# Two trunk layers in split float32: four plain feature tiles instead of six, the pre-norm of the other half in nine slots, the convolution's input moved

## What is computed

```python
for i in range(DEPTH):
    hn = rmsnorm(x, mix_pre_g[i])
    y = pool_mixer(hn, ...) if i % 2 == 0 else mlstm_mixer(hn, ...)
    x = x + rmsnorm(y, mix_post_g[i])
    hn = rmsnorm(x, ffn_pre_g[i])
    a = jax.nn.relu(hn @ mlp_w1[i])
    x = x + rmsnorm((a * a) @ mlp_w2[i], ffn_post_g[i])
```

## Time and profile before

| | |
|---|---|
| median of 3 runs | 1963.46 us (1962.75 to 1964.49) |
| the profiled execution | 1964.01 us |
| its span, first to last instruction | 1962.2 us |
| TensorE matmul, weight load | 1926.7 us (98%), 1542.1 us (79%) |
| VectorE, ScalarE, POOL | 1344.6 us (69%), 1067.7 us (54%), 89.9 us (5%) |
| granted TensorE clock, mean | 0.993 |

### The profile page before, as it was taken

How to read it: one execution, slowest core, us unless ns; L and a number is a source line. 1 busy time by engine, 2 the same in 40 slices (tenths; PEclk the granted TensorE clock), 3 DMA queues, 4 the chain that set the end, 5 groups by cost and what they waited for, 6 DMA issues and landing times. The chain is left out here.

```text
span 1962.2 us, 24457 instructions
## 1 busy us (share of the span) xinstructions
PE 1926.7 (98%) x8526; PEld 1542.1 (79%) x8526; DVE 1344.6 (69%) x2120; ACT 1067.7 (54%) x1825; POOL 89.9 (5%) x121
## 2 busy tenths in 40 slices
PE   9999999999999999999999999999999999999999
PEld 6678888888788788778878778877888888878876
DVE  5777565655678977775866766777665656577885
ACT  7655555553445446666655656745645455435433
POOL 0110000000000100110000110011000000000010
PEclk9999999999999999999999999999999999999999
DMA  5344343447633633342323343235334345753353
GB/s 210 109 163 155 118 177 118 177 179 298 214 92 92 200 106 106 110 151 87 99 85 97 111 147 100 83 119 185 115 146 149 146 149 215 294 187 97 103 188 128
DMA packets 79706, 285.00 MB, mean 145 GB/s; under 512 B 9408, under 2 KB 9536, under 8 KB 71136
## 3 DMA queue, kind: packets, MB, share of 16 engines
q1 hardware_dynamic: 64288, 239.96, 34.9%
q0 software_dynamic: 8320, 27.27, 4.3%
q10 hardware_dynamic: 6976, 16.21, 2.8%
HBM read 211.51 MB, written 71.89 MB: 144 GB/s over the span
## 5 line engine op out<-in xcount | busy, mean ns | idle before, releaser
L1821 DVE TENSOR_TENSOR w_lo<-raw,w_hi 128x1024 fp32r<-128x1024 f32 x132 | 162.6, 1232 | 152.6 <-ACT w_hi L1281 150.2
L1467 ACT CAST h_hi<-h_raw 128x512 fp32r<-128x512 f32 x188 | 116.5, 620 | 246.7 <-PE core L1022 149.1
L803 PE MATMUL bank<-x_hi,w_hi 128*128 128x512 f32 x560 | 228.5, 408 | 1.7 <-issue 1.2
L1281 ACT CAST w_hi<-raw 128x1024 fp32r<-128x1024 f32 x132 | 137.6, 1043 | 163.4 <-PE bank L805 52.3
L805 PE MATMUL bank<-x_hi,w_lo 128*128 128x512 f32 x560 | 223.4, 399 | 0.0
L804 PE MATMUL bank<-x_lo,w_hi 128*128 128x512 f32 x560 | 222.2, 397 | 0.0
L2076 DVE TENSOR_TENSOR h_lo<-h_raw,h_hi 128x512 fp32r<-128x512 f32 x188 | 129.8, 690 | 120.8 <-ACT h_hi L1467 120.5
L1020 PE MATMUL core<-h_hi,w_hi 128*128 128x512 f32 x464 | 183.3, 395 | 0.6 <-DVE y L2142 0.6
L1021 PE MATMUL core<-h_lo,w_hi 128*128 128x512 f32 x464 | 183.5, 396 | 0.0
L1022 PE MATMUL core<-h_hi,w_lo 128*128 128x512 f32 x464 | 183.3, 395 | 0.0
L1970 DVE TENSOR_TENSOR w_lo<-sums,w_hi 128x512 fp32r<-128x512 f32 x104 | 71.8, 690 | 100.4 <-ACT w_hi L1309 97.5
(11 more groups left out here) (334 smaller groups left out, 4411.2 us busy)
## 6 DMA issues: line engine op xcount, KB each, us to landing
raw<-weights SPq DMA_DIRECT2D x132, 512.0 KB, 3.3
h_pair_dram<-y SPq DMA_DIRECT2D x26, 1792.0 KB, 6.7
h_raw<-h_pair_dram SPq DMA_DIRECT2D x182, 256.0 KB, 2.8
w<-second_pairs SPq DMA_DIRECT2D x24, 768.0 KB, 4.4
raw_odd<-first_pairs SPq DMA_DIRECT2D x14, 1024.0 KB, 7.1
x_scratch<-y POOLq DMA_DIRECT2D x48, 256.0 KB, 2.5
raw<-first_pairs SPq DMA_DIRECT2D x12, 1024.0 KB, 7.1
xold<-x_scratch POOLq DMA_DIRECT2D x40, 256.0 KB, 3.5
```

Source lines behind the costliest of these rows:

```text
L803: nc.tensor.matmul(o, a, hi(t), start=(k == 0), stop=False)
L1281: nc.scalar.copy(w_hi[:, ROW[u] * T:(ROW[u] + 2) * T], raw[:, (n % RAW) * BLK:(n % RAW + 1) * BLK]).then_inc(hi_ready, 1)
L1467: nc.scalar.copy(h_slot(n)[0], h_raw[:, at % H_RAW, :]).then_inc(h_hi_ready, 1)
L1821: dve.tensor_tensor(w_lo[:, s], raw[:, (n % RAW) * BLK:(n % RAW + 1) * BLK], w_hi[:, s].bitcast(F32), ALU.subtract).then_inc(lo_ready, 1)
```

## The change

Six tiles become four, thirteen pairs fourteen. The chain's slots move from 1 to 11 to 0 to 8; the sums of the input quadrants move with the shorter front; the sets of banks for odd and even pairs are swapped; the early weights of the second product go to the other buffer. In the heads, `conv_input(j, 1)` goes right behind `decay_matrix(j - 1)`, block (j,3) is cast ahead of `query(j)`, and VectorE does `conv(j, 1)` ahead of that block's low part. In the second product, the chain for the MLP's half 0 starts one step earlier and its last part takes three iterations.

```diff
-PLAIN = 6
+PLAIN = 4
 PAIRS = (F_TILES - PLAIN) // 2
...
-W2_FROM = (0, 4, 7, 10, PAIRS)
+W2_FROM = (0, 4, 7, 11, PAIRS)
...
         def pair_banks(i):
-            return bank[0:3] if i % 2 else core[0:3]
+            return core[0:3] if i % 2 else bank[0:3]
...
             if n < AHEAD:
-                return raw[:, n * T:(n + 1) * T]
+                return raw_odd[:, n * T:(n + 1) * T]
...
         FIRST_SLOTS = {
-            "root_post": {1: 1}, "recip_post": {1: 1},
-            "residual": {2: (0, 1), 3: (2, 3), 4: (4, 5), 5: (6, 7)},
-            "square": {2: (0,), 3: (1, 2), 4: (3, 4), 5: (5,), 6: (6, 7)},
-            "add": {3: (0, 1), 4: (2, 3), 5: (4,), 6: (5, 6), 7: (7,)},
-            "root_pre": {8: 1}, "recip_pre": {8: 1},
-            "normed": {8: (0, 1, 2), 9: (3, 4, 5), 10: (6, 7)},
-            "high": {9: (0, 1, 2), 10: (3, 4, 5), 11: (6, 7)},
-            "low": {9: (0, 1), 10: (2, 3, 4), 11: (5, 6, 7)},
+            "root_post": {0: 1}, "recip_post": {0: 1},
+            "residual": {0: (0,), 1: (1, 2), 2: (3, 4), 3: (5, 6, 7)},
+            "square": {1: (0, 1), 2: (2, 3), 3: (4, 5), 4: (6, 7)},
+            "add": {2: (0, 1), 3: (2, 3), 4: (4, 5), 5: (6, 7)},
+            "root_pre": {6: 1}, "recip_pre": {6: 1},
+            "normed": {6: (0, 1, 2, 3), 7: (4, 5, 6, 7)},
+            "high": {7: (0, 1, 2, 3, 4, 5), 8: (6, 7)},
+            "low": {7: (0, 1, 2, 3), 8: (4, 5, 6, 7)},
...
-        RESIDUAL_AT = (P3_AT - 1, P3_AT + 3, P3_AT + 4, P3_AT + 6, P3_AT + 7, P3_AT + 9, P3_AT + 10, P3_AT + 11)
+        RESIDUAL_AT = (P5_AT + 11, P3_AT + 3, P3_AT + 4, P3_AT + 6, P3_AT + 7, P3_AT + 9, P3_AT + 10, P3_AT + 11)
...
-                loads(b0, b0 + FRONT - 4)
+                loads(b0, b0 + FRONT - 2)
                 pair_load(layer, 0)
-                loads(b0 + FRONT - 4, b0 + FRONT)
+                loads(b0 + FRONT - 2, b0 + FRONT)
...
-                    if s < 2 * PLAIN:
+                    if s <= 2 * PLAIN:
                         chain_slot(5 if layer else 1, FIRST_SLOTS, s)
-                    elif s - 2 * PLAIN in (1, 2, 4):
-                        input_high(layer, (1, 2, 4).index(s - 2 * PLAIN))
+                    else:
+                        input_high(layer, s - 2 * PLAIN - 1)
...
                     decay_matrix(j - 1)
+                    conv_input(j, 1)
                     tick(j, 0)
+                    split_hi(BLOCK["head", j, 2] + 1)
                     query(j)
                     if j % HEADS:
                         rows_to_all(j)
-                    split_hi(BLOCK["head", j, 2] + 1)
                     tick(j, 1)
-                    conv_input(j, 1)
...
                     if t < 0:
                         chain_slot(5 if layer else 1, FIRST_SLOTS, s)
-                    elif t in (0, 1, 3, 5):
-                        input_sum(layer, (0, 1, 3, 5).index(t))
-                    if t in (2, 4, 5):
-                        input_low(layer, (2, 4, 5).index(t))
-                    if t == 4:
+                    else:
+                        if t == 0:
+                            chain_slot(5 if layer else 1, FIRST_SLOTS, s)
+                        input_sum(layer, t)
+                    if t > 0:
+                        input_low(layer, t - 1)
+                    if t == PLAIN - 2:
                         pair_sums(layer, 0, 0)
                         pair_sums(layer, 0, 1)
...
                     states(j - 1)
+                    conv(j, 1)
                     split_lo(BLOCK["head", j, 2] + 1)
                     tick(j, 1)
-                    conv(j, 1)
                     denominators(j - 1)
```

More of the change, by code:

```diff
@@ L115, in w2_chunk @@
     return max(c for c in range(W2_CHUNKS) if W2_FROM[c] <= i)
-def pairs_before(layer, i):
-    return layer * ((PAIRS + 1 - i % 2) // 2) + i // 2
 def step_of(n):
@@ L347, in build @@
             h_lo = arena.enter_context(nc.sbuf_tensor("h_lo", [P, H_RING, T], F32R))
-            arena.enter_context(nc.sbuf_tensor("not_used", [P, 6 * T], F32))
+            arena.enter_context(nc.sbuf_tensor("not_used", [P, 2 * T], F32))
             h_raw = arena.enter_context(nc.sbuf_tensor("h_raw", [P, H_RAW, T], F32))
@@ L643, in build @@
                          P5_AT + 5: (4,), P5_AT + 6: (5,), P5_AT + 7: (6,), P5_AT + 8: (7,)},
-            "root_post": {P3_AT - 2: 1}, "recip_post": {P3_AT - 2: 1},
+            "root_post": {P5_AT + 10: 1}, "recip_post": {P5_AT + 10: 1},
             "residual": {at: (k,) for k, at in enumerate(RESIDUAL_AT)},
@@ L647, in build @@
             "add": {at + 2: (k,) for k, at in enumerate(RESIDUAL_AT)},
[L648 to L651, removed]
+            "root_pre": {N1_AT: 1}, "recip_pre": {N1_AT: 1},
+            "normed": {N1_AT: (0,), N1_AT + 1: (1, 2, 3), N1_AT + 2: (4, 5, 6, 7)},
+            "high": {N1_AT + 1: (0, 1), N1_AT + 2: (2, 3, 4), N1_AT + 3: (5, 6, 7)},
+            "low": {N1_AT + 2: (0, 1), N1_AT + 3: (2, 3, 4, 5, 6, 7)},
         }
@@ L689, in pairs_stored @@
                 for s in range(2):
-                    sp.wait_ge(pair_stored[s], 16 * (pairs_before(layer, s) + (i + 2 - s) // 2))
+                    sp.wait_ge(pair_stored[s], 16 * (layer * PAIRS // 2 + (i + 2 - s) // 2))
             def hidden_load(layer, n):
@@ L715, in mlp @@
                 split_done(PAIR[layer, PAIRS - 2, "P4"][0])
-                sp.dma_start(raw[:, :].rearrange("p (i t) -> p i t", i=AHEAD),
+                sp.dma_start(raw_odd[:, :].rearrange("p (i t) -> p i t", i=AHEAD),
                              w_second[layer, A11, :, 0:AHEAD, :]).then_inc(early_landed, 16)
@@ L739, in mlp @@
                     if m == 0:
-                        split_done(STEP[layer, AHEAD - 1][0])
+                        split_done(PAIR[layer, PAIRS - 1, "P4"][0])
                     if 0 <= m < PLAIN:
@@ L942, in pairs_first @@
                             pe.wait_ge(t_ready, 4 * layer + {"P5": 1, "P7": 2, "P6": 3, "P4": 4}[name])
-                        if i == 1 and name in ("P1", "P5", "P2"):
+                        if i == 0 and name in ("P1", "P5", "P2"):
                             b = ("P1", "P5", "P2").index(name)
                             pe.wait_ge(plain_taken, layer * HALVES * PLAIN + plain_of_bank(layer, b, 1) + 1)
-                        if i == 0 and name == "P1":
+                        if i == 1 and name == "P1":
                             pe.wait_ge(part_copied, (layer + 1) * KT)
@@ L1302, in pair_hi @@
                 if src < S1:
-                    act.wait_ge(pair_landed[i % 2], 16 * (pairs_before(layer, i) + 1))
+                    act.wait_ge(pair_landed[i % 2], 16 * (layer * PAIRS // 2 + i // 2 + 1))
                     of = pair_raw(i)[:, src * T:(src + 1) * T]
@@ L1427, in pairs_first @@
                         if i >= 2:
-                            act.wait_ge(pair_stored[i % 2], 16 * pairs_before(layer, i))
+                            act.wait_ge(pair_stored[i % 2], 16 * (n // 2))
                         nc.scalar.copy(y[i % 2][:, H_ROW["P1"], :], x[:, :]).then_inc(p1_copied, 1)
@@ L1466, in hidden_hi @@
                     act.wait_ge(group_done, PAIR[layer, PAIRS - 1, "P4"][1])
+                    act.wait_ge(lo_ready, STEP[layer, AHEAD - 1][0] + 1)
                 nc.scalar.copy(h_slot(n)[0], h_raw[:, at % H_RAW, :]).then_inc(h_hi_ready, 1)
@@ L1490, in second_out @@
                         for s in range(2):
-                            act.wait_ge(pair_stored[s], 16 * pairs_before(layer + 1, s))
+                            act.wait_ge(pair_stored[s], 16 * (layer + 1) * PAIRS // 2)
                     for d in range(4):
@@ L1945, in pair_sums @@
                 n = layer * PAIRS + i
-                dve.wait_ge(pair_landed[i % 2], 16 * (pairs_before(layer, i) + 1))
+                dve.wait_ge(pair_landed[i % 2], 16 * (n // 2 + 1))
                 of = pair_raw(i)
```

## The result

The changed kernel takes **1991.22 us** (median of four runs, 1988.66 to 1992.14); the kernel before took 1963.64 us beside it. The ratio is **1.0139** (95% interval 1.0123 to 1.0156): slower, inside the range, 7.5 us above the forecast. The profiled execution took 1988.66 us, the fastest of the four, with a span of 1986.9.

A forecast was written before the change was run, and what follows sets the result against it. TensorE, busy 98% of 1962.2 us, was taken as the bound. Terms -11.2 + 17.1 + 20.5 + 2.0 - 6.5 - 8.5 + 6.8 = +20.2 us on the profiled 1964.0 gave 1984.2, less 0.5 for the median: 1983.7 us, range 1969 to 1998.

The forecast's parts named there:

- Matmuls: Two plain tiles become one pair: 24 fewer matmuls a layer, 48 in all, -11.2 us on TensorE's path.
- The rest at zero: Pair banks, early second weights, load chunks and second product's chain slots cost nothing; bounds -0.5 to +1.5 us.
- The fronts: MLP fronts with 12 steps instead of 18: TensorE waits on VectorE's chain, +17.1 us layer 0, +20.5 us layer 1.
- VectorE with idle time between slots 0 and 8: Sign of a wrong forecast: idle time on VectorE within the fronts' norm chain; no size given.
- Behind step 8 and the clock: After the long front wait: late load of block 10, +2.0 us in all, and half clock, +6.8 us in all.
- The term of 3.4 us a layer for the clock: Each 12.4 us front wait leaves one half-clock dip that is not covered: 3.4 x 2 = +6.8 us.
- The heads: Earlier convolution input cuts hnorm waits, adds 2.6 us in head 8: waits 7.2 against 13.7 us, -6.5 us.
- at half clock half the stretch is lost: 11.9 us: Four half-clock stretches behind head waits cost 1.7 + 3 x 3.4 us, all regained when the dips go.
- A: Rival: front waits at their lower bound, heads gain fully except head 8; about 1967 to 1972 us, chance 0.14.
- B: Rival: all head waits and dips go, front wait below 18 us per layer; 1954 us, chance 0.08.
- C: Rival: long waits leave doubled dips of 6.8 us, 1.5 us head waits dip too; 1997 us, chance 0.12.
- D: Rival: the fronts' chain is not on the path, only matmul and convolution gains count; 1938 us, chance 0.01.

The follow-up runs named there:

- e4: Changed kernel with chain slot 8 done first on ScalarE and VectorE, ahead of step 8's bank copies and block 9's split: 1979.98 us, ratio 1.0084.
- e8: Changed kernel with the four 512-column reciprocals of the fronts' chains replaced by plain copies: 1978.31 us, ratio 1.0075.
- e6: Changed kernel with four fp32 matmuls on constants, results unread, put into TensorE's wait for hn_ready: 1991.46 us, ratio 1.0145.
- e1: Kernel before with only the heads' convolution of block (j,1) moved, on both engines: 1953.95 us, ratio 0.9953.
- e3: Kernel before with ScalarE's convolution copy moved in every head, VectorE's convolution in all but heads 0 and 8: 1949.95 us, ratio 0.9931.
- e3 again: The kernel of e3 run once more, beside e9 on the same chip: 1950.68 us, ratio 0.9931.
- e7: e3 with the seventh residual of the heads' chains one slot later, one fewer ahead of the denominators in heads 4 and 12: 1952.89 us, ratio 0.9946.
- e9: e3 with the heads' norm chain ungrouped, residuals, squares and sums spread over more blocks: 1947.83 us, ratio 0.9920.
- e2: Changed kernel with the heads' convolution put back where it was: 1999.36 us, ratio 1.0182.

## Why the prediction was right, and where its sizes were off

**Matmuls.** Right: 120 more in the pairs and the second product cost 28.4 us in layer 1, for 28.1. In layer 0 it was 30.8. "The rest at zero" is the step that failed there: TensorE waits for VectorE ahead of the last sum, 0.69 and 0.55 us at 716 and 720 us, and in the first pair for ScalarE, 0.78 us before 168.6. All of it belongs to the shorter front and its pairs: the stretch took 574.1 to 575.0 us in all six kernels with four plain tiles and 544.0 in all six with six tiles; the 574.1 is e4's, which doesn't have the wait in the first pair. For the waits at 716 us one cause is to be seen: the pre-norm's sum on POOL now falls beside a weight split. POOL:

```profile
707.45 3.23 POOL L1239 PARTITION_ALL_REDUCE tot<-acc  x1 [3.24 <-DVEq L1886]
```

and VectorE:

```profile
708.35 2.41 DVE L1817 TENSOR_TENSOR w_lo<-raw,w_hi 128x1024 fp32r<-128x1024 f32 x1 [1.06 <-ACT w_hi L1276]
```

The split took 2.41 us instead of 1.22. No run tried this part alone; that it makes these waits is argued, not shown, and it can't be all of the 2.7 us.

**The fronts.** Right in sum (+20.6 us of waits and clock in layer 0 for +21.5, +24.8 in layer 1 for +24.9), but the sum is in part luck: two misses of opposite sign. From step 1 to step 8 the forecast was 2.1 us too low in layer 0 and 2.2 in layer 1; behind step 8 it was 2.3 and 1.6 too high. Of the first miss 1.5 us a layer are the loads of old x: VectorE stood idle 2.96 and 2.97 us for them, where the forecast had 1.5 for all eight. Another idle time that the forecast doesn't have are 1.69 us ahead of the low part at 111.6 us, for ScalarE, which did two squares first. "VectorE with idle time between slots 0 and 8" stood among the signs of being wrong, and VectorE was idle 12.3 us in each layer; about 7 us of that the forecast had itself in its sum (1.5 for the loads, 3 for POOL's sum, 2.8 for ScalarE in step 8). So the sign came true in part: the chain through VectorE is the bound, and not VectorE's work alone.

From matmul to matmul, less the 0.23 us that are always there: step 2 waited 1.7 and 6.9 us (forecast 1.9 and 6.9), step 5 3.5 and 2.0 (2.8), step 8 10.2 and 10.9 (12.4). Step 8 waited less because TensorE came to it later: half clock behind the waits of step 5 (from 106.2 us for 6.8 us) and of step 2 in layer 1 (from 1314.5 us for 10.2 us, and 3.4 more from 1341.8) slowed it while VectorE went on. A load of old x held VectorE 1.76 us ahead of step 5 in layer 0 (the row at 105.85 above) and 1.63 us in layer 1; in layer 1 the wait was shorter all the same, since TensorE had come later. e8 shows the chain through VectorE as the cause, e4 ScalarE's order in step 8 as the addition.

**Behind step 8 and the clock.** The forecast had 1.0 + 3.4 us a layer there; 24.61 and 25.30 us against 22.5 for 96 matmuls give 2.1 and 2.8. The term of 3.4 us a layer for the clock was the one that was wrong in kind: the forecast called these two stretches "not covered", and e6 shows layer 0's covered whole and 0.7 us of layer 1's bare. What covers them is what the forecast priced beside it at 0 to 2.5 us, and took at 1: block 10, forecast 8 us behind `hn_ready`, could be used 8.8 us behind it, and with VectorE's work after that it makes the whole 2.1 us. No run loads block 10 earlier, so what that would save is not shown. The granted clock there, columns as in rows 4:

```profile
130.10:140.30 10.20, 2.91 (x7) 2.33 (x8) 6.67 (x7) 5.96 (x11) 0.00 (x0) 0.50 0.50 193
...
1362.30:1376.00 13.70, 6.22 (x15) 4.87 (x16) 6.88 (x8) 6.16 (x12) 0.00 (x0) 0.50 0.58 218
```

They last 10.2 and 13.7 us, longer than any of rows 4, but most of that lies in the wait itself. The Trainium skill, "TensorE: Matmul & The Clock Gate", section "HAM oscillation", warns of the work behind a long wait. The trace agrees that the clock falls; e6 shows that here it costs 0 and 0.7 us.

**The heads: +4.6 us of the miss.** The waits were sized well: 0.4 us in heads 2 and 10 (forecast 0.6 and 0.7), 1.7 in heads 4 and 12 (1.5 and 1.6), 3.2 in head 8 where 0.7 had been (+2.5 for +2.6), and e1 and e3 show their causes. The term that failed is "at half clock half the stretch is lost: 11.9 us". In heads 4 and 12 the slow stretch of the kernel before hid a wait right behind it. TensorE in head 4, kernel before:

```profile
867.61 1.11 PE L1132 MATMUL core<-consts,hnorm 128*128 128x128 f32 x4 [3.04 <-DVE hnorm L2278]
...
876.79 0.39 PE L803 MATMUL bank<-hid_hi,w_hi 128*128 128x512 f32 x1
```

and after:

```profile
877.48 0.66 PE L1127 MATMUL core<-consts,hnorm 128*128 128x128 f32 x4 [1.56 <-DVE hnorm L2276]
...
885.90 0.47 PE L798 MATMUL bank<-hid_hi,w_hi 128*128 128x512 f32 x1 [1.39 <-issue]
```

Before, 9.18 us from the one to the other, 6.3 of them at half clock, and no wait; after, full speed and 8.42 us, since the block's split comes too late. Of 3.1 us only 0.8 is gained, and as much in head 12. The two traced executions of e3, one kernel on two chips, show it without an edit: in head 4 the first kept full speed, and in e3 again the clock fell to half from 863.3 us for 3.4 us. TensorE of e3, with the wait at the next block, and then that block's first matmul in e3 again:

```profile
860.33 0.66 PE L1132 MATMUL core<-consts,hnorm 128*128 128x128 f32 x4 [1.57 <-DVE hnorm L2278]
...
868.74 0.47 PE L803 MATMUL bank<-hid_hi,w_hi 128*128 128x512 f32 x1 [1.40 <-issue]
```

```profile
869.88 0.47 PE L803 MATMUL bank<-hid_hi,w_hi 128*128 128x512 f32 x1
```

It is 8.41 us at full speed with a wait, and 8.42 us (from 861.46) with half clock and none. Behind the wait are ScalarE's square, which waits for VectorE, and the split after it; e7 made this wait longer and e9 shorter, so the queue is shown. The four dips gave back 1.5, 0.7, 2.1 and 0.8 us by the offsets of the two traces, 5.1 for 11.9. Head 8's own dip held TensorE up by 2.3 us, but an idle time of 0.52 us at the next product went for it, and 1.3 us were left, for 3.4. With the waits (-9.5 + 2.5) that makes -10.8, for a measured -10.4; most of the rest is a new wait at the second block of the heads (0.28 us idle before 742.8 us).

**The rivals.** A (the front at its lower bound) fell: the waits were at the forecast, though a better order (e4) goes 8 to 11 us towards it. B needed less than 18 us of wait a layer; with the clock there were about 20 and 25. C (dips doubled and head waits dipping) fell by its price: the dips behind the long waits were longer but covered, and the waits of 1.7 us kept the clock at 1.00 in this execution. They don't always keep it: in e3 again, e4 and e8 the clock fell for 3.4 us behind the same wait in head 4, in e6 behind the one in head 12, and e3 shows that it cost nothing. So the prediction's line between waits of 3 us and more, which fell, and shorter ones, which did not, doesn't hold: half clock stands behind step 5's wait of 2.0 us in layer 1 too (from 1341.8 us), and in the kernel before it stands, from 68.4 us, behind a wait of 2.19 us that ended at 66.9. D fell. The rule of the Trainium skill ("SBUF — State Buffer", "SBUF: two separate sides"), by which the hold in head 2 could reach 3.2 us, met another VectorE operation than in the kernel before:

```profile
815.88 1.59 DVE L2263 SCALAR_TENSOR_TENSOR small<-small 128x4 f32<-128x4 f32 x1
```

An operation that takes 0.16 us elsewhere took 1.59 us beside the sum that POOL began at 815.21 and, by the trace, ended at 818.44: a hold of 1.4 us, nearer to the row's 1.9 than to the rule's 3.2, and it was over 1.0 us before the sum.

## What to carry to other kernels

Before taking work away from the engine that bounds the whole, add up what another engine must do in the same stretch: here 48 matmuls less (-11.2 us) shortened the only place in which the chain could hide, and the kernel with that change alone was 36 us slower (e2). Count the idle times of that other engine too, and what each is for: here loads of old x, POOL's sum, ScalarE's queue, and a load of weights that waits for the end of the chain. A stretch at half clock is worth half its length only if nothing is late behind it: look at which operand the engine would wait for next. Work moved out of the way of one deadline should be followed to the next one (e7), and a part of a change is worth trying without the one place where it hurts (e3, e9: 12 to 15 us faster than before).

## What was not expected of the hardware

Half clock doesn't end with the wait that brought it: without work it lasted to 140.3 us in the changed kernel, 2.9 us into the new work; with the eight matmuls in the wait (e6) it was over at 135.8 us, ahead of the work at 139.3. Whether the clock falls at one and the same short wait differs from run to run: at 68 us it fell in the kernel before and in e3 again, and not in the changed kernel or in e9, and the runs differ by about 1.8 us in the start of step 1 for it. Small effects of an edit have to be read from stretches that begin behind such a place. Another such place is the front of layer 1, which is the same code in the six kernels with six plain tiles: from step 0 it took 104.8 to 105.5 us in three traced executions and 107.9 to 108.1 in the others (e1, e3, e7). In e1 VectorE waits there 1.79 us for old x before 1326.25 us; TensorE then waits 2.0 us, and the clock is at half for 3.4 us behind it.
